# Prompt attention: order of the samples' latent queries and the first head's scores, placement of the exponential's table load, and spreading of the rope queries

## The reference, cut to what matters

```python
q_nope, q_rope = q[..., :64], _rope(q[..., 64:], pos)          # 16 heads, 64 + 32
# prompt: keys and values are made from the latent, causal softmax over 512 keys
k = concat(einsum('bkc,chn->bkhn', c_lat, w_uk), k_rope)
o = causal_attention(concat(q_nope, q_rope), k, einsum('bkc,chv->bkhv', c_lat, w_uv))
# samples: queries go to the latent space, keys are 2048 cached rows (latent 256 + rope 32) and the new ones
q_lat = einsum('bqhn,chn->bqhc', q_nope, w_uk)
o_lat = causal_attention(concat(q_lat, q_rope), keys, keys[..., :256])
o = einsum('bqhc,chv->bqhv', o_lat, w_uv)
```

## Time and profile before

| | |
|---|---|
| three runs | 2255.33, 2255.96, 2258.66 us; median 2255.96 us |
| profiled execution | 2255.74 us, of which 2254.0 us are the span |
| TensorE clock granted, mean | 0.997 |
| busy share of the span | PE 98%, PEld 88%, DVE 52%, ACT 39%, POOL 29% |
| chain of work that ended last | PE 96%, DVE 2%, ACT 1% |

### The profile page before, as it was taken

How to read it: one execution, slowest core, us unless ns; L and a number is a source line. 1 busy time by engine, 2 the same in 40 slices (tenths; PEclk the granted TensorE clock), 3 DMA queues, 4 the chain that set the end, 5 groups by cost and what they waited for, 6 DMA issues and landing times.

```text
span 2254.0 us, 42639 instructions
## 1 busy us (share of the span) xinstructions
PE 2210.7 (98%) x16239; PEld 1981.8 (88%) x16239; DVE 1170.6 (52%) x1831; ACT 874.9 (39%) x1815; POOL 655.1 (29%) x316
## 2 busy tenths in 40 slices
PE   7999999999999999999999999999999999999998
PEld 5899997667789999999988999966677999999998
DVE  4443753844346666651153717457443476666433
ACT  4223225832234555541132332366322355555322
POOL 0223433400022333333322334342000323333332
PEclk9999999999999999999999999999999999999999
DMA  9554332033333222235545333212332422222332
GB/s 302 170 145 100 85 85 66 19 109 108 85 130 91 79 84 84 84 109 167 173 126 176 83 97 83 79 43 63 97 108 57 156 70 83 79 80 83 87 85 84
DMA packets 338278, 230.69 MB, mean 102 GB/s; under 512 B 62732, under 2 KB 321605, under 8 KB 338140
## 3 DMA queue, kind: packets, MB, share of 16 engines
q1 hardware_dynamic: 336594, 226.37, 35.1%
q10 hardware_dynamic: 1546, 2.43, 0.4%
HBM read 223.15 MB, written 5.60 MB: 101 GB/s over the span
## 4 chain that ended last, share of the span: by engine, by line
PE 96%; DVE 2%; ACT 1%; DMA 0%; issue 0%; DVEq 0%; SPq 0%; ACTq 0%
PE PS L1550 62%; PE PS L1518 7%; PE PS L2000 5%; PE PS L2047 5%; PE PS L1912 3%; PE PS L1833 2%; PE PS L1646 2%; PE PS L1594 2%; PE PS L1936 2%; PE PS L1567 1%; PE PS L1889 1%; PE PS L1994 1%; PE PS L1950 1%; PE PS L2076 0%; DMA rows_in<-x_sample 0%
## 5 line engine op out<-in xcount | busy, mean ns | idle before, releaser
L975 POOL TENSOR_TENSOR wlo<-raw,whi 128x1024 fp32r<-128x1024 f32 (+1 forms) x248 | 586.0, 2363 | 1493.5 <-ACT whi L563 1493.5
L1550 PE MATMUL PS<-h_hi,whi 128*128 128x288 f32 x2496 | 740.7, 297 | 1.2 <-issue 1.0
L1550 PE MATMUL PS<-h_hi,wlo 128*128 128x288 f32 x2496 | 737.1, 295 | 0.0
L1550 PE MATMUL PS<-h_lo,whi 128*128 128x288 f32 x2496 | 737.0, 295 | 0.0
L563 ACT ACTIVATE whi<-raw 128x1024 fp32r<-128x1024 f32 (+1 forms) x252 | 258.4, 1025 | 919.6 <-PE PS L1550 823.5
L1550 PEld LDWEIGHTS PS<-h_hi,whi 128*128 128x128 f32 x2496 | 470.9, 189 | 9.4 <-issue 8.8
L1550 PEld LDWEIGHTS PS<-h_lo,whi 128*128 128x128 f32 x2496 | 471.0, 189 | 0.2
L1550 PEld LDWEIGHTS PS<-h_hi,wlo 128*128 128x128 f32 x2496 | 470.5, 188 | 0.0
L1452 DVE TENSOR_SCALAR conv<-zext,convp 128x592 f32<-128x592 f32 x88 | 153.6, 1746 | 132.5 <-ACTq L894 132.1
L1550 PE MATMUL PS<-act_hi,whi 128*128 128x288 f32 x704 | 209.9, 298 | 0.0
L1550 PE MATMUL PS<-act_hi,wlo 128*128 128x288 f32 x704 | 207.8, 295 | 0.0
(11 more groups left out here) (288 smaller groups left out, 3410.8 us busy)
## 6 DMA issues: line engine op xcount, KB each, us to landing
raw<-w_up SPq DMA_DIRECT2D x88, 512.0 KB, 3.8
pages<-cache_latent SPq DMA_DIRECT2D x256, 144.0 KB, 2.1
raw<-w_in SPq DMA_DIRECT2D x64, 512.0 KB, 4.0
ada_ring<-w_ada SPq DMA_DIRECT2D x41, 512.0 KB, 4.9
raw<-w_down SPq DMA_DIRECT2D x32, 512.0 KB, 3.9
ada_next<-w_ada SPq DMA_DIRECT2D x17, 512.0 KB, 4.0
ada_first<-w_ada SPq DMA_DIRECT2D x16, 512.0 KB, 10.4
raw<-w_out SPq DMA_DIRECT2D x16, 512.0 KB, 4.5
```

Of the source, the lines that this page charges most:

```text
L975: nc.gpsimd.tensor_tensor(wlo[:, slot, 0:n], raw[:, slot, 0:n], whi[:, slot, 0:n].bitcast(F32), ALU.subtract).then_inc(lo_ready.sem, 1)
L1550: r = mm(PS[0:m, 2 * (j % pairs) + half, 0:HT], w, o[:, k0 + k, half * HT:half * HT + HT], start=(first and k == 0 and part is whi and o i ...
```

## The change

There are four edits in each layer.

1. PE: the 32 products of the latent queries stand behind `head_scores(0)`, ahead of `head_scores(1)`.
2. ACT: behind the two first `head_query` stands an exponential of one column (of `eps`, into an unused column of `softm`), in front of which the compiler now puts the table load; then come head 0's exponentials, then the copies to `qlat`.
3. DVE: `causal_row` is filled right after the rope of the queries, ahead of the wait for the values; the four copies to `qrs[0:32]` stand behind `maxima(0)`, ahead of `normalised(0)`, and raise the new signal `qrs_own`.
4. The three copies after head 3 are gone from DVE. SP, behind sample 0's pages, waits for `qrs_own` and issues three DMAs from `qrs[0:32]` to the other groups (signal `qrs_in`), for which PE waits where it waited for `qrs_ready`.

```diff
@@ -289,7 +289,8 @@
     lat_T, lat_ev = signal("lat_T", 5), signal("lat_ev", 5)
     last_ready, last_T, last_ev = signal("last_ready", 1), signal("last_T", 1), signal("last_ev", 1)
     y_ready, q_roped, gated = signal("y_ready", 4), signal("q_roped", 1), signal("gated", KD, 2)
-    qlat_p, qlat_ev, qrs_ready = signal("qlat_p", 1), signal("qlat_ev", 1), signal("qrs_ready", 1)
+    qlat_p, qlat_ev, qrs_in = signal("qlat_p", 1), signal("qlat_ev", 1), signal("qrs_in", 3 * 16)
+    qrs_own = signal("qrs_own", 1)
 
     q_asm, k_asm, k_rope = signal("q_asm", NH), signal("k_asm", NH), signal("k_rope", 2)
     qk, smax, expd, normed = signal("qk", 4 * NH), signal("smax", 4 * NH), signal("expd", 4 * NH), signal("normed", NH)
@@ -482,6 +483,9 @@
                     sp.wait_ge(tab_in.sem, 16)
                 sp.wait_ge(unit_used.sem, unit_used.at(l, U_OUT))
                 keys_of(0)
+                sp.wait_ge(qrs_own.sem, qrs_own.at(l, 1))
+                for r in range(1, 4):
+                    sp.dma_start(qrs[32 * r:32 * r + 32].rearrange("p b h s -> p (b h s)"), qrs[0:DR].rearrange("p b h s -> p (b h s)")).then_inc(qrs_in.sem, 16)
                 sp.wait_ge(qlat_p.sem, qlat_p.at(l, 1))
                 sp.wait_ge(k_asm.sem, k_asm.at(l, NH))
                 keys_of(1)
@@ -784,6 +788,8 @@
 
                 head_query(0)
                 head_query(1)
+                nc.scalar.activation(softm[:, 44:45], eps[:, 0:1], ACT.Exp)
+                exponentials_of(0)
                 act.wait_ge(qlat_p.sem, qlat_p.at(l, 1))
                 for c in range(KC):
                     for g in range(2):
@@ -791,7 +797,8 @@
                                                     PS[:, 4 + 2 * c + g, :].rearrange("p (h b s) -> p h b s", h=8, b=NB), ACT.Copy)
                 last.then_inc(qlat_ev.sem, 1)
                 for h in range(NH):
-                    exponentials_of(h)
+                    if h > 0:
+                        exponentials_of(h)
                     if h > 0:
                         turned_probs(h - 1)
                     if h + 2 < NH:
@@ -1293,6 +1300,8 @@
                     v.tensor_tensor(qr[:, t, :], qr[:, t, :], tmp[:, 0, :], ALU.add)
                     v.drain()
                 v.drain().then_inc(q_roped.sem, 1)
+                v.memset(causal_row[:, 0:TP - 128], 0.0)
+                v.tensor_copy(causal_row[:, TP - 128:TP], causal[:])
 
 
 
@@ -1300,9 +1309,10 @@
                 dve.wait_ge(free["uv"].sem, free["uv"].at(l, 4))
                 for s in range(2):
                     v.tensor_copy(k96[DN:96, s, :], krope[:, 0:TP]).then_inc(k_rope.sem, 1)
-                for j in range(4):
-                    v.tensor_copy(qrs[0:DR].rearrange("p b (t j) s -> p j t b s", j=4)[:, j], qr[32 * j:32 * j + 32, :, TP:T].rearrange("p t (b s) -> p t b s", b=NB))
-                v.drain()
+                def own_queries():
+                    for j in range(4):
+                        v.tensor_copy(qrs[0:DR].rearrange("p b (t j) s -> p j t b s", j=4)[:, j], qr[32 * j:32 * j + 32, :, TP:T].rearrange("p t (b s) -> p t b s", b=NB))
+                    v.drain().then_inc(qrs_own.sem, 1)
 
                 def maxima(h):
                     for qb in range(4):
@@ -1328,18 +1338,13 @@
                     gb = gate_b[:, p, 0:TP]
                     v.tensor_tensor(gb, gb, PS[:, 7, :], ALU.mult).then_inc(o_done.sem, 1)
 
-                v.memset(causal_row[:, 0:TP - 128], 0.0)
-                v.tensor_copy(causal_row[:, TP - 128:TP], causal[:])
-                v.drain()
                 for h in range(NH):
                     maxima(h)
+                    if h == 0:
+                        own_queries()
                     if h >= 3 and h % 2 == 1:
                         out_pair(h // 2 - 1)
                     normalised(h)
-                    if h == 3:
-                        for j in range(1, 4):
-                            last = v.tensor_copy(qrs[32 * j:32 * j + 32], qrs[0:DR])
-                        last.then_inc(qrs_ready.sem, 1)
 
                 def rope_keys(b):
                     dve.wait_ge(kt_p.sem, kt_p.at(l, 5 * b + 1))
@@ -1892,13 +1897,6 @@
                     if n % 2 == 1:
                         nc.tensor.drain().then_inc(unit_used.sem, 1)
 
-                pe.wait_ge(lat_ev.sem, lat_ev.at(l, 5))
-                for h in range(NH):
-                    p, s = h // 2, 64 * (h % 2)
-                    for c in range(KC):
-                        r = mm(PS[:, 4 + 2 * c + h % 2, 64 * p:64 * p + 64], wukT[s:s + 64, p, 128 * c:128 * c + 128],
-                               qn[s:s + 64, p, TP:T], start=True, stop=True)
-                r.then_inc(qlat_p.sem, 1)
 
 
                 def head_scores(h):
@@ -1966,6 +1964,13 @@
                 banks_free_of(l, "uv")
                 pe.wait_ge(k_rope.sem, k_rope.at(l, 2))
                 head_scores(0)
+                pe.wait_ge(lat_ev.sem, lat_ev.at(l, 5))
+                for h in range(NH):
+                    p, s = h // 2, 64 * (h % 2)
+                    for c in range(KC):
+                        r = mm(PS[:, 4 + 2 * c + h % 2, 64 * p:64 * p + 64], wukT[s:s + 64, p, 128 * c:128 * c + 128],
+                               qn[s:s + 64, p, TP:T], start=True, stop=True)
+                r.then_inc(qlat_p.sem, 1)
                 for h in range(NH):
                     if h + 1 < NH:
                         head_scores(h + 1)
@@ -2075,7 +2080,7 @@
                     pe.wait_ge(spt_d.sem, spt_d.at(l, 3 * b + 3))
                     mm(PS[:, 7, 0:KVL], pT[0:TS, NPG, :], newk[:], start=False, stop=True).then_inc(spv.sem, 1)
 
-                pe.wait_ge(qrs_ready.sem, qrs_ready.at(l, 1))
+                pe.wait_ge(qrs_in.sem, qrs_in.at(l, 3 * 16))
                 all_scores(0)
                 for b in range(1, NB):
                     all_scores(b)
```

## The result

The changed kernel takes 2262.03 us, the median of ten runs (2259.36 to 2267.63), against 2256.06 us for the kernel before in ten runs of its own (2255.33 to 2258.66). The ratio is 1.003 (95% interval 1.0021 to 1.004). It is slower by about 6 us, where I forecast 0.3 and a range that ended at 2259.0. The profiled execution took 2261.49 us, with a span of 2259.7 us: 5.7 more than before.

A forecast was written before the change was run, and what follows sets the result against it. PE held 96% of the chain. Per layer -2.2 (copies) + 0.95 (ACT's start) + 1.4 (clock) = +0.15 us, +0.3 for two layers, gave 2256.3 us against the median of 2255.96; range 2252.5 to 2259.0 us.

The forecast's parts named there:

- clock, 1.4 us a layer, bounds 0.9 to 1.7: Start of prompt attention: PE's longer pause drops the clock over head 0's scores and latent queries, 1.4 us a layer.
- rival (c): Low clock after the pause lasts a second stretch (2259.7 us), or through head 1's scores (8.3 a layer, 2270 us); 6%.
- the low stretch of before: Over head 0's transposes, 385.2 to 388.5: lower clock, claimed not on the path, so its going gives nothing back.
- The three copies (-2.2 a layer): After head 3: without DVE's copies the pair falls from 11.17 to 8.95 us, gaining 2.2 us a layer.
- rival (d): Head 4: the copies' 2.2 us don't come back because PE waits elsewhere; 2260.7 us, chance 3%.
- ACT's start-up (+0.95): Start of attention: ACT's new order delays the first pair values by 0.95 us a layer, bounds 0.4 to 1.5.
- Rival (a): The clock holds through PE's pause ahead of head 0's scores: -1.25 us a layer, 2253.5 us; chance 24%.
- DVE's copies to `qrs[0:32]`: Behind head 0's maxima: covered by 0 to 0.6 us, as transposes need `qlat_ev`; up to 2.4 without cover.
- The table load: Start of attention: ACT loads the table while waiting for head 0's scores, so 1.28 us leaves the path.
- (b): Head 0's earlier exponentials (1.3 us) carry through, latent queries not in ACT's way: -3.5 a layer, 2249.0 us; 7%.
- The signs I named: Trace marks around the start of attention, such as first pair values 21.2 us after the last values, 18.8 before.

The follow-up runs named there:

- e1: The kernel before with only DVE's three copies after head 3 replaced by three DMAs from SP; 2252.23 us, ratio 0.9979.
- e4: The kernel before with only the latent queries moved behind head 0's scores on PE; 2278.72 us, ratio 1.0101.
- e5: The kernel before with SP's three DMAs in place of DVE's copies after head 3, and the early table load on ACT; 2248.29 us, ratio 0.9959.
- e9b: e2 with DVE's four copies to `qrs[0:32]` back ahead of head 0's maxima; 2247.76 us, ratio 0.996.
- e3: The changed kernel with 32 identity transposes on PE filling the pause ahead of head 0's scores; 2252.85 us, ratio 0.9982.
- e2: The changed kernel with the latent queries back ahead of head 0's scores on PE; 2253.31 us, ratio 0.9985.
- e7: The changed kernel with 32 identity transposes on PE between head 0's scores and the latent queries; 2264.99 us, ratio 1.0032.

## Why the prediction was wrong

**The step that failed** is the term "clock, 1.4 us a layer, bounds 0.9 to 1.7", and with it the 6% of rival (c). The fall itself was right: in the pause I named, just ahead of head 0's scores (377.99 where I had 378.9). What failed is how long it lasts. I took the length of the low stretch, 3.4 us, from the two that the kernel before shows. Those were followed by score products and 128 x 128 transposes. In the new order the latent queries follow, and of them no low stretch of before says anything. In layer 1 the cost was 1.70, my upper bound. In layer 0 it was 6.98. That is rival (c) in its longer form, which I had given a part of 6%, in one of two layers. That layer 1 came within my bounds is no proof of the reasoning: there the clock fell later and was back before the latent queries began. Its 8.3 us is the work from 379.5 on at half speed; 2.27 + 3.30 + 2.40 = 7.97 were lost on PE, of which 0.99 would have gone to ACT anyway.

**The argument against (c) was the weak place.** I wrote that after the low stretch of before, during which PE was busy, the clock was back at once. A busy PE turned out not to be enough: in layer 0 it was busy for 3.40 of 3.40 us in four rows that all stand at 0.50.

**A reading that was wrong beside it.** I wrote that the low stretch of before was not on the path. The chain of before has nothing but PE from head 1's scores to the first pair values, the ten transposes among it with 1.74 us:

```profile
383.63 3.73 PE PS L1912 x8
...
389.11 2.16 PE PS L1912 x8
...
392.36 2.26 PE PS L1912 x8
```

e1 bears this out with 20.09 against 19.01 us, and so do the 27 runs of before beside e1 to e4: nine at a mean clock of 0.995 took 2257.86 us or more, the two at 0.998 took 2254.13 and 2254.60. It did not spoil the forecast, since the new start-up was worked out from ACT's list and not by what this stretch would give back. But it hid a gain that e5 and e9b then found.

**The pause and the page.** The Trainium skill speaks against the edit, as the prediction said: page "TensorE: Matmul & The Clock Gate", section "Part 1: The HAM clock gate". It was right about the pause. But it gives the clock back once PE has been busy for a while. Layer 1 agrees, with full clock after 3.4 us of score products; layer 0 doesn't, with 17.1 us.

**The three copies (-2.2 a layer)** were right. From pair values to pair values it is 8.96 us instead of 11.17, a gain of 2.21. e1 shows it alone (8.96 in both layers), and rival (d) is out.

**ACT's start-up (+0.95)** was right: +0.99 in e3, where the changed order runs at full clock. Rival (a) forecast 2253.5 us and 19.8 us to the first pair values; e3, which is the changed kernel with the clock held, has 2252.85 and 19.90. The us to the pair values are the safer comparison: against the 2257.47 beside it e3 is 4.6 us faster, where (a) has 2.5. So the sum was sound in every term but one. In the changed kernel itself the term was hidden in layer 0 behind the slow PE.

**DVE's copies to `qrs[0:32]`** were covered in the changed kernel, as I claimed with a margin of 0 to 0.6 us and a cost of up to 2.4 without the cover. e2 takes the cover away, and e9b takes the copies out of the way: 0.9985 to 0.996. Their profiles show the wait of 2.68 us shrink to 0.91, and the low clock go. The forecast had the cover from `qlat_ev`; in layer 1 PE itself was busy with head 1's scores for longer still, until 1500.5, with the normalisation done at 1499.0.

**The table load** left the path as forecast, but in the changed kernel that brings nothing, since ACT waits for `qlat_p` behind it. Where the order of PE is left alone, it is worth 1.0 to 1.2 us a layer, the low stretch that went with it included (e5). I had this rival's price, 1.3, under (b), and tied it to PE's new order, which it didn't need.

**The signs I named.** Head 0's scores at the old distance: 3.71 us, near it. Copies to `qlat` 7.5 us behind the start of the scores: 11.7 in layer 0, 7.9 in layer 1. First pair values at 21.2: 21.60 in layer 1, 26.88 in layer 0 (I had counted from 0.07 us behind the evacuation). Head 1's exponentials 3 us later against the values than before, without idle time ahead: 2.9 in layer 1, 6.7 in layer 0, no idle time in either. Nine us between the pair values, and no wait at the samples' rope scores: right.

**What stays open.** In layer 1 of the changed kernel the clock fell 4.05 us behind the last product of the values and was back before the latent queries; in layer 0 it fell 2.89 us behind it and met them. Why it falls sooner in one layer than in the other is open, and so is what in the latent queries keeps it low. In e4 the layers are the other way round, so it is not the layer. The ten runs of the changed kernel, from 2259.36 us at a mean clock of 0.995 to 2267.63 at 0.990, show that it also differs from run to run. I have no edit that steers it, only those that avoid it (e3, e5, e9b).

## What to carry to other kernels

Moving work out of a wait of TensorE makes the wait a pause, and the price of the pause is not its length but the clock of all that follows on the path: 6.98 us for 3.75 here. Before giving a queue another order, look at what stands behind the new pause, and if it is small products, count the case in which all of it runs at half speed as a likely one. Of a change of four edits, test each alone: here one gives 5 us, one (its early table load) gives 2 to 4 where PE's order is left alone, one is hidden or costs 5 by where the others stand, and one costs 9 with the others and 21 by itself.

## What the runs showed of the hardware

- A PE that is busy without a gap can stay at the lower clock: 3.40 of 3.40 us busy in four rows in a row, with products of 64 rows by 64 columns in three of them. The stretch was 13.7, 17.1 and 20.5 us long in the three cases in which these products met the low clock (in the one of 20.5, PE also paused for 4.02 us). With 32 transposes of 128 x 128 ahead of them it was 6.8 at most (e7), and 6.8 also over scores and transposes alone with PE busy throughout (e1, layer 0).
- fp32 transposes by the identity can keep the clock up: 32 of them, 3.71 us, held it in both layers (e3).
- The same instructions can meet a long or a short low stretch from one layer to the next (17.1 and 3.4 us in the changed kernel), so two equal observations of one length, as in the kernel before, are not a bound.
